# Eight-core gMLP and convolution trunk: x passed twice, once transposed and cast by the load itself

## What is computed

```
layer 0: h = gelu(x @ w_in + b_in); u, v = halves of h (2048 columns each)
         v = layer_norm(v); per 128 positions and head group: v = W_masked @ v + b_s
         x = layer_norm(alpha*x + (u*v) @ w_out + b_out)
layer 1: b, c, h = x @ w_in3 (1024 columns each); h = causal conv of width 3 over c*h
         x = layer_norm(alpha*x + (b*h) @ w_out)
after each mixer: x = layer_norm(alpha*x + relu(x @ w1)**2 @ w2)     (4096 hidden columns)
```

## Time and profile before

| | us |
|---|---|
| median of 3 runs | 1403.59 (1402.45 to 1602.96) |
| profiled execution, span of the slowest core | 1402.3 |
| spans of the eight cores in it | 1391.4 to 1402.3 |
| PE busy in it | 1370.6 (98%) |
| DVE, ACT, POOL busy | 1041.6, 673.8, 206.3 |

### The profile page before, as it was taken

How to read it: one execution, slowest core, us unless ns; L and a number is a source line. 1 busy time by engine, 2 the same in 40 slices (tenths; PEclk the granted TensorE clock), 3 DMA queues, 4 the chain that set the end, 5 groups by cost and what they waited for, 6 DMA issues and landing times.

```text
span 1402.3 us, 18833 instructions; the slowest of 8 cores (1391.4 to 1402.3 us)
## 1 busy us (share of the span) xinstructions
PE 1370.6 (98%) x6924; PEld 658.5 (47%) x6924; DVE 1041.6 (74%) x1975; ACT 673.8 (48%) x1206; POOL 206.3 (15%) x390
## 2 busy tenths in 40 slices
PE   6999999999999999999999899999999999999997
PEld 3444445444465445444444354544444644544443
DVE  3476778867788687976775858788677876788767
ACT  3645367236352276146364553760646324840732
POOL 0141022012001102111102311210210110111100
PEclk8999999999999999999999999999999999999999
DMA  8998249389335559598999751782963465775502
GB/s 191 149 153 142 36 65 150 57 138 147 63 57 85 105 85 155 84 152 134 176 207 191 111 90 30 113 143 47 166 104 61 69 111 84 113 121 91 120 1 120
DMA packets 102236, 154.92 MB, mean 110 GB/s; under 512 B 52864, under 2 KB 52864, under 8 KB 102144
## 3 DMA queue, kind: packets, MB, share of 16 engines
q0 software_dynamic: 46608, 112.74, 51.4%
q1 hardware_dynamic: 55536, 40.98, 12.3%
HBM read 246.49 MB, written 8.39 MB: 182 GB/s over the span
## 4 chain that ended last, share of the span: by engine, by line
PE 79%; DMA 15%; DVE 2%; issue 2%; POOL 1%; SPq 0%; ACT 0%; DVEq 0%; POOLq 0%; ACTq 0%
PE ps L464 50%; PE ps L450 22%; DMA wq<-wbig 7%; PE ps L589 6%; DMA xres<-x 2%; DMA ws<-wsm 1%; DMA xT<-xb 1%; DMA xT<-wq 1%; PE ps L901 1%; DMA out<-xres 1%; DMA lnc<-rows 1%; DMA wq<-x 1%; POOL st L661 0%; DVE wq L879 0%; DVE xT L625 0%
## 5 line engine op out<-in xcount | busy, mean ns | idle before, releaser
L450 PE MATMUL ps<-xT,ws 128*128 128x512 f16 (+1 forms) x2000 | 377.5, 346 | 11.0 <-DVE H L907 6.8
L450 PEld LDWEIGHTS ps<-xT,ws 128*128 128x128 f16 x2000 | 193.9, 98 | 170.4 <-issue 17.0
L464 PE MATMUL ps<-wq,sc 128*128 128x512 f16 x1184 | 270.2, 379 | 0.0
L464 PE MATMUL ps<-wq,H 128*128 128x512 f16 x888 | 206.0, 379 | 0.0
L407 POOL DMA_DIRECT2D ws<-wsm x208 | 112.7, 543 | 501.5 <-PE ps L450 166.3
L464 PEld LDWEIGHTS ps<-wq,sc 128*128 128x128 f16 x1184 | 115.9, 98 | 139.7
L744 DVE SCALAR_TENSOR_TENSOR xres<-xres,ps 128x512 f32<-128x512 f32 x192 | 129.9, 684 | 61.4 <-PE ps L464 47.1
L464 PE MATMUL ps<-xT,ws 128*128 128x512 f16 x624 | 152.5, 379 | 0.0
L674 ACT ACTIVATE xb<-xres,st 128x1024 bf16<-128x1024 f32 x64 | 73.0, 1140 | 143.7 <-DVE st L671 140.1
L464 PEld LDWEIGHTS ps<-wq,H 128*128 128x128 f16 x888 | 86.8, 98 | 104.3
L417 ACT ACTIVATE ps<-ps 128x512 f32<-128x512 f32 x89 | 51.9, 583 | 163.2 <-PE ps L464 150.0
(11 more groups left out here) (112 smaller groups left out, 1523.9 us busy)
## 6 DMA issues: line engine op xcount, KB each, us to landing
wq<-wbig POOLq DMA_DIRECT2D x104, 512.0 KB, 7.2
ws<-wsm POOLq DMA_DIRECT2D x208, 256.0 KB, 5.4
lnc<-rows SPq DMA_DIRECT2D x20, 512.0 KB, 7.1
xres<-x SPq DMA_DIRECT2D x16, 512.0 KB, 7.0
out<-xres SPq DMA_DIRECT2D x15, 512.0 KB, 7.1
sc<-rows SPq DMA_DIRECT2D x8, 256.0 KB, 6.3
wq<-x POOLq DMA_DIRECT2D x3, 512.0 KB, 7.1
sc<-rows POOLq DMA_DIRECT2D x2, 512.0 KB, 8.9
```

What stands on the lines that cost most here:

```text
L450: ins = e.matmul(bk.buf[:, p * n * 128:(p + 1) * n * 128], ws.buf[:, kc, :], xT[:, kc, t0 * 128:(t0 + n) * 128], start=(kc == 0 and not be ...
L464: ins = e.matmul(bk.buf[:], lhs(kc), rhs(kc), start=(first and kc == 0), stop=(kc == nk - 1), skip_group_check=True)
```

## The change

x is passed to the kernel a second time as `xt`: for each tile of 128 positions a block of 128 partitions (features within a chunk) by eight chunks of 128 positions, f32. `load_xT` casts a tile of it straight into `xT`, whose layout becomes tile, chunk, position; all readers and writers of `xT` follow.

- In the first half the tiles of `xt`, the weights of v's column blocks 0 and 1 are loaded by POOL, unpaced, in the order tile 0, block 0 (two loads), tiles 1 to 7, block 1 (three loads). The f32 tiles of x are loaded later, behind the first u block of the second quarter, and `add_bout` moves behind them.
- The weights of column block 1 are laid out anew in HBM: two quarters of 128 columns by full depth, then 256 columns by full depth. `v_second` computes the block in these pieces, in the first half tile by tile in four tiles for each quarter.
- The first v block is emitted as two operations of four matmuls. The seed no longer waits for `xT` of the tile before.
- 27 warm-up matmuls instead of 16. Columns, gains, identity and the constant of `rstd` are set up after column block 1 (`init_late`, the lines moved out of `init`).
- In the second half, eight loads of `xt` replace five casting loads and eight DMA transposes.

```diff
-        xT = sb("xT", [128, 8, TH], LP)
+        xT = sb("xT", [128, NT, 8, 128], LP)
...
-                                       xT[:, kc, t0 * 128:(t0 + n) * 128], start=(kc == 0 and not begun),
+                                       xT[:, t0:t0 + n, kc, :], start=(kc == 0 and not begun),
...
-        def load_x(h, tt, paced=True):
+        def load_x(h, tt, after=()):
...
+        def load_xT(h, tt, paced=True):
+            dma_cast(lambda: xT[:, tt, :, :].rearrange("p c t -> p (c t)"), xt_ap[h * NT + tt],
+                     [("xT", tt, c) for c in range(8)], ("xt", tt), 128 * 4096, paced)
...
+            for i in range(NWARM):
...
+            def v_second():
+                (wa, wb), flat = av[1], (lambda v: v.buf[:].rearrange("p a b -> p (a b)"))
+                quarter = lambda q: (lambda kc: flat(wa)[:, q * 1024 + kc * 128:q * 1024 + (kc + 1) * 128])
+                first = lambda kc: flat(wa).rearrange("p (q k c) -> p q k c", q=2, k=8)[:, :, kc, :]
+                last = lambda kc: flat(wb)[:, kc * 256:(kc + 1) * 256]
+                a_keys, b_keys, banks = [(wa, 0), (wa, 1)], [(wb, 0)], {}
+                if h > 0:
+                    for tt in range(NT):
+                        bk = v_seed(1, 0, 512)
+                        v_mm(bk, tt, 0, 256, first, range(8), a_keys)
+                        v_mm(bk, tt, 256, 256, last, range(8), b_keys)
+                        v_act(1, tt, bk, 0, 512)
+                        v_stats(1, tt)
+                    return
+                for q in range(2):
+                    for tt in range(4):
+                        if q == 0:
+                            banks[tt] = v_seed(1, 0, 256)
+                        v_mm(banks[tt], tt, q * 128, 128, quarter(q), range(8), [a_keys[q]])
+                        if q == 1:
+                            v_act(1, tt, banks[tt], 0, 256)
+                for tt in range(4, NT):
+                    bk = v_seed(1, 0, 256)
+                    v_mm(bk, tt, 0, 256, first, range(8), a_keys)
+                    v_act(1, tt, bk, 0, 256)
+                for tt in range(NT):
+                    bk = v_seed(1, 256, 256)
+                    v_mm(bk, tt, 0, 256, last, range(8), b_keys)
+                    v_act(1, tt, bk, 256, 256)
+                    v_stats(1, tt, (0, 256))
...
             if h == 0:
-                load_x(0, 0, False)
-            load_av(0)
+                load_xT(0, 0, False)
+            load_av(0, h > 0)
             if h == 0:
                 for tt in range(1, NT):
-                    load_x(0, tt, tt > 1)
-            load_av(1)
+                    load_xT(0, tt, False)
+            load_av(1, h > 0)
+            V += [vt("wq") for tt in range(NT)]
...
-                if h == 0:
-                    transpose_x(tt)
-                v_block(0, tt)
+                v_block(0, tt, h == 0 and tt == 0)
             load_av(3)
-            for cb in (1, 2):
-                for tt in range(NT):
-                    v_block(cb, tt)
+            v_second()
+            if h == 0:
+                init_late()
+            for tt in range(NT):
+                v_block(2, tt)
...
             ao = load_blocks(BIG_BASE["a_out"])
+            if h == 0:
+                for tt in range(NT):
+                    load_x(h, tt, [("H", 4, 0)])
+                add_bout()
...
-                    for tt in (0, 1, 2, 4, 6):
+                    for tt in range(NT):
                         load_xT(1, tt)
```

More of the change, by code:

```diff
@@ L350 @@
 PLAIN = 3
+NWARM = 27
 def build_nc():
@@ L764, in load_xT @@
[L764 to L779, removed]
@@ L791, in init @@
             add("dve", lambda e: e.tensor_copy(ident[:], tmp.buf[:, 0:128]), reads=[tmp], writes=["ident"], dur=0.2)
-            add("dve", lambda e: e.memset(ones_bf[:], 1.0), writes=["ones"], dur=0.2)
             add("dve", lambda e: e.memset(neghalf[:], -0.5), writes=["neghalf"], dur=0.2)
[L794 to L800, removed]
-                    add("pe", lambda e, bk=bk: e.matmul(bk.buf[:], ones_bf[:], zero.buf[:, 0, :], start=True, stop=True),
-                        reads=["ones", zero], writes=[bk, "warm"], dur=0.43)
         def init_gate():
@@ L847, in gate_mixer, with v_seed @@
             V, sts = [], [vt("st") for tt in range(NT)]
             v16 = lambda tt, a, b: V[tt].buf[:].rearrange("p a b -> p (a b)")[:, a:b]
[L850 to L854 removed]
+            def v_seed(cb, a, n):
+                bk, row, o = vt("ps"), rows[cb // 2], cb % 2 * 512 + a
+                add("act", lambda e: e.activation(out=bk.buf[:, 0:n], in_=row.buf[:, o:o + n], func=AF.Copy),
+                    reads=[(row, cb % 2)], writes=[bk], dur=t_act(n, True))
+                return bk
@@ L856, in mm, with v_mm @@
+            def v_mm(bk, tt, c0, n, rhs, kcs, reads):
                 def mm(e):
-                    for kc in range(8):
-                        ins = e.matmul(bk.buf[:], xT[:, kc, tt * 128:(tt + 1) * 128], av[cb][kc // 4].buf[:, kc % 4, :],
-                                       start=False, stop=(kc == 7), skip_group_check=True)
-                    return ins
-                add("pe", mm, reads=av[cb] + [("xT", tt, c) for c in range(8)], writes=[bk], dur=8 * T_MM)
-                s, a, b = sts[tt], cb * 512, (cb + 1) * 512
@@ L863, in v_block @@
-                add("act", lambda e: e.activation(out=v16(tt, a, b), in_=bk.buf[:], func=AF.Gelu), reads=[bk],
-                    writes=[(V[tt], cb)], dur=t_act(512), table="gelu")
-                add("dve", lambda e: e.bn_stats(s.buf[:, 6 * cb:6 * cb + 6], v16(tt, a, b)), reads=[(V[tt], cb)],
-                    writes=[(s, cb)], dur=0.69)
+                    for kc in kcs:
+                        ins = e.matmul(bk.buf[:, c0:c0 + n], xT[:, tt, kc, :], rhs(kc), start=False, stop=(kc == 7),
+                                       skip_group_check=True)
@@ new lines, in mm, with v_act, v_stats @@
+                    return ins
+                add("pe", mm, reads=reads + [("xT", tt, c) for c in range(8)], writes=[bk],
+                    dur=len(kcs) * T_MM * n / 512)
+            def v_act(cb, tt, bk, c0, n):
+                a = cb * 512 + c0
+                add("act", lambda e: e.activation(out=v16(tt, a, a + n), in_=bk.buf[:, 0:n], func=AF.Gelu), reads=[bk],
+                    writes=[(V[tt], cb, c0)], dur=t_act(n), table="gelu")
+            def v_stats(cb, tt, parts=(0,)):
+                s, a = sts[tt], cb * 512
+                add("dve", lambda e: e.bn_stats(s.buf[:, 6 * cb:6 * cb + 6], v16(tt, a, a + 512)),
+                    reads=[(V[tt], cb, c0) for c0 in parts], writes=[(s, cb), (V[tt], cb)], dur=0.69)
@@ L943, in gate_mixer @@
                     load_x(h, tt)
-            add_bout()
+                add_bout()
             for q in range(1, 4):
```

82 lines of the change are left out of this document (49 added, 33 removed).

## The result

The changed kernel takes **1393.24 us** (median of 4 runs, 1391.56 to 1425.11) against 1403.62 for the kernel before in the same rounds: ratio **0.9919 [0.9899, 0.994]**, 10.4 us less, no change by the 2% of this measurement. Run again on another chip it gave 1393.31 us (1392.43 to 1395.03), ratio 0.9926 [0.9904, 0.9948]. Medians are over all runs; ratios leave out runs in which cores were granted a lower clock. The forecast of 1394 is met. Its sum is not: the start gave less than half of its term, the second half three times its own.

The account below looks back on a forecast made before the run. PE was taken as the bound (busy 1370.6 of 1402.3 us), DMA engines as second limit. Terms -8.5 + 1.4 - 2.6 = -9.7 us gave a span of 1392.6, plus 1.3 to the median: 1394 us, range 1384 to 1403.

Parts of the forecast that it names:

- the start: v's first three column blocks: the third ends at 57 us instead of 65.6, 8.5 us earlier.
- the second half: DMA transposes leave the stretch before the second gate stage; two short PE waits of 0.7 and 1.9 us credited, 2.6 us.
- the 192nd: v's 192nd matmul of 512 columns, the end of the third column block; expected near 57 us.
- rival 1: The gain at the kernel's start is lost to the clock or the loads: 1397, up to 1401 us; chance 0.20.
- The first weights: POOL's first loads: column block 0's second weights, with two bias rows beside them, land at 14.6 us as before.
- rival 4: First-half xt casts land one after the other at 3.8 us each: 1406 us; chance 0.04.
- The clock: PE's first matmuls after 27 warm-ups: granted clock taken as kept, with a loss of 3.0 us as upper end.
- The first gate: First gate stage: its load chain comes 7.1 us earlier against PE's 8.5, so 1.4 us are given back waiting.
- f32 x later: Eight f32 x loads near 98 us, 14.5 us on SP, covered by idle DMA time: cost taken as nothing.
- Pieced reads of xT: PE matmuls streaming xT in four pieces of 128 columns: cost taken as 0, upper end 19.8 us.
- rival 3: Reading xT in pieces costs PE time in both halves' F-type products: 1414 us at full price; chance 0.05.
- Rival 2: Loads relieve both gate stages, all 6.8 us of waits for the gate's multiply go, nothing given back: 1386 us; chance 0.14.

Follow-up runs that it names:

- experiment 9: Changed kernel with bias rows 1 to 3 held until x tiles 0, 2, 3 and the s row until the third column block's second weights landed: 1390.09 us.
- experiment 8: Changed kernel again, unaltered: 1393.31 us; beside it, bias rows held until x tiles 0, 2, 3 and the s row until tile 7: 1391.03 us.
- experiment 7: Changed kernel with column block 1 undivided, 512 columns at a time, weights in two loads: 1397.12 us, ratio 0.9956 to the kernel before.
- experiment 5: Changed kernel with bias rows 1 to 3 held until x tiles 2, 4, 6 landed and the s row until tile 7: 1393.24 us, ratio 0.993.
- Experiment 4: Changed kernel with the first half's f32 x loads and bias adds moved back early, run twice; second run 1402.27 us, ratio 0.9987 to the kernel before.
- Experiment 1: Changed kernel with the first half as before, keeping the new xT layout and the second half's eight xt loads: ratio 0.9958 to the kernel before.
- experiment 3: Changed kernel with eight DMA transposes of zeros into unused buffers added as ballast: 1401.32 us in the profiled run, no ratio.
- experiment 2: Changed kernel with the second half's x loaded as before, by five casting loads and eight DMA transposes: ratio 0.9984 to the kernel before.

## Why the number was right and its terms were not

Terms on core 2: -8.5 + 1.4 - 2.6 forecast; measured -3.4 at the 192nd, -0.6 at the first gate, +0.2 between, -8.6 at the second gate, 12.4 of the 12.5 us of span. Two errors, 5.1 too much at the start and 6.0 too little in the second half, cancelled: that the number came out is luck. By its own signs the start went rival 1's way: the first v matmul came at 15.45 us, not by 11, and the clock was 0.50 after 15 us.

- **The first weights (the step that failed at the start).** "Now one tile of xt stands ahead of the two blocks in POOL's queue, and two rows of biases beside them: about as many bytes, so I keep 14.6 us." There were four rows: `load_av` for column blocks 2 and 3 adds its row too, and nothing on SP stood ahead of it once x was gone from there. The second weights landed at 19.15 us on core 2. Over all cores they landed at 18.1 to 19.3 us in the two profiles of the changed kernel, and at 14.6 to 16.8 in the four with rows 1 to 3 held; there the 192nd came about 1.5 us sooner (medians of the cores 60.4 us in experiment 9, 61.9 in the changed kernel of experiment 8). That is shown. The landings of one execution don't tell how far the rest, over 14.6, is due to the row that stayed or to the 13 casts issued back to back.
- **The xt tiles.** Forecast 1.81 us apart; the seven landed from 20.5 to 30.3 us, 1.63 apart. Right, and rival 4 is out. By the fixed cost that the Trainium skill (DMA: Bandwidth & Descriptors, "Anatomy of one DMA — SWDGE (gpsimd) path") puts into each DMA, about 2 us, they couldn't come so close one after the other; here that part overlaps.
- **The clock.** "I take the new clock as kept." It fell. At the full clock PE would have caught up with the xt tiles and waited for the second, which landed at 20.5 us; seven blocks of 1.73 us behind it end at 32.6, my estimate from these landings. The block ended at 34.3, so 1.7 us are the clock's, within the 3.0 bound of rival 1. The last tile (forecast 27.3 + 1.7) would not have set the end of block 0 either way: 29.0 became 32.6 by the late weights and tiles and 34.3 by the clock.
- **Column blocks 1 and 2.** 14.0 and 13.8 us forecast, 14.0 and 13.8 measured. Right, and experiment 7 shows what the pieces spare.
- **The first gate.** The chain was to come 7.1 us earlier and PE 8.5; they came 4.0 and 3.4 earlier. The sign of the small rest turned: 0.6 won, not 1.4 given back. That a gain of PE is kept only as far as the loads follow is half right: in experiment 5 all eight cores wait there again (0.9 to 3.5 us), but in experiment 9, with the start 1.5 us earlier, none does.
- **f32 x later.** Costed at nothing, and no wait for it appears: the eight loads leave at 119.6 to 130.5 us and land within 7.4 us, with the DMA share at 0.96 where it was 0.69, and DVE carries the adds:

```profile
120.00:150.00 30.00, 30.00 (x197) 15.88 (x195) 25.76 (x34) 17.05 (x29) 3.69 (x7) 1.00 0.96 216
```

  What I had not seen is what it buys. Experiment 4 puts it at 9.0 us, since the x tiles now come twice.
- **Pieced reads of xT.** L454 of after against L450 of before, from section 5 of the two pages: 2000 matmuls each, no cost, and rival 3 is out. The kernel before is busy 2.7 us more there; the slow matmuls behind its second gate's wait are 2.9.

```profile
L454 PE MATMUL ps<-xT,ws 128*128 128x512 f16 (+1 forms) x2000 | 374.8, 344 | 5.1 <-DVE H L944 2.5
```

```profile
L450 PE MATMUL ps<-xT,ws 128*128 128x512 f16 (+1 forms) x2000 | 377.5, 346 | 11.0 <-DVE H L907 6.8
```

- **The second half (mis-sized the other way).** "I credit the two short waits ... The longest of L907's (3.5 us of the 6.8) I leave, as bounded by 0 and 3.5." It went whole, and with it 2.9 us of half clock behind it, a price that stood in no term: waits were counted, what PE does after them was not. Rival 2 came true for the second gate and not for the first. Experiment 1 shows that it comes from the second half's own part, the chain in experiment 3 that on the slowest cores a transpose's landing stood ahead of the loads.

## What to carry over

Price a wait with the slow matmuls behind it: two waits of 5.4 us at the second gate were worth 8.3. When loads are put in order of need, go through every queue that starts at time zero; rows on another queue take the same engines. And when an operand is passed a second time, the first copy's load has to leave the stretch, or the saving is lost.

## What the hardware showed beyond that

- Granted clock: kept on two cores of the 53 warm-ups run through waits of 3.1 to 3.3 us, half for 10.2 us on core 2 of after from within a wait of 5.75, and half for 6.8 to 10.2 us on every core of experiment 9, whose waits there were 3.7 at most. No run here separates what decides.
- In the first run of experiment 4 all cores were granted 0.81 for 153 to 162 us, cores 2 and 3 of experiment 2 for 159 us: a level between the other two. In the second run of experiment 4 core 7 has 1.00 in the stretch in which the first has this:

```profile
100.00:200.00 100.00, 100.00 (x478) 46.37 (x477) 61.27 (x95) 43.17 (x72) 16.19 (x29) 0.81 0.54 87
```

- Where SP's rows and POOL's casts left together, the four rows landed at 6.4, 7.2, 12.7 and 16.7 us, the first tile at 10.65: the queues share the engines, and order within one says little about landings across two.
